# Hybrid decoder layer on one core: gating values computed token-major, and copies, residual additions, sums and a store placed elsewhere in the engines' programs

## The chip, the cores and the metric

The kernel runs on one core of a Trainium2 chip. The metric is the device time of one execution in microseconds (us). The engines are TensorE (PE, matrix products; PEld is its loading of stationary operands), VectorE (DVE), ScalarE (ACT), GpSimd (POOL) and SyncE (SP, which here only issues DMA transfers).

## The reference

A decoder layer over 512 tokens of width 2048, all in float32. What matters here:

```python
h = rmsnorm(x, norm_mix_g)
q, kv, nsa_g, u, v, merge_g = split(h @ w_in)          # v: 512 tokens x 1024
o_a = nsa_attention(...)                               # 16 heads
v = layernorm(gelu(v), ln_g, ln_b)                     # statistics over the 1024 values of a token
mixed = einsum('gts,bcsgd->bctgd', tril(ws), v)        # 8 groups of 128 values, chunks of 128 tokens
o_b = gelu(u) * (mixed + b)
x = x + (sigmoid(g0) * (o_a @ w_proj_a) + sigmoid(g1) * (o_b @ w_proj_b)) @ w_mix_out
x = x + cross_attention(rmsnorm(x), rmsnorm(mem))
gt, up = split(rmsnorm(x) @ w_ffn_in)                  # hidden width 5632
x = x + (silu(gt) * up) @ w_ffn_out
return rmsnorm(x, norm_final_g)
```

## The kernel before

**Precision.** Products are made in fp32r with both operands split into a high part and a low remainder: hi x hi, hi x lo and lo x hi are added in PSUM. ACT or DVE makes the high part (a copy to fp32r), DVE the remainder (a subtraction). A weight panel is 2048 x 128, loaded to `raw` in two slots and split by quarters (4 blocks of 128 rows) into `w_hi` and `w_lo`, which hold four quarters. PSUM has 8 banks of 128 x 512 float32.

**Order.** Each engine has its own program, written out by hand; semaphores tie them together, and a count says how far another engine must have come. An engine that waits holds everything behind it in its program. `Phase` keeps the counts: panels, quarters (`split_done` by DVE, `quarters_done` by PE) and groups (a group is one result in a bank, `banks_read` says that it was copied out). Most phases use banks 0 and 1 in turn.

**The stages that the change touches.**

- *merge, then sv.* While attention runs (banks 2 to 7), PE also makes 32 panels of merge gates in banks 0 and 1; ACT copies each to `gate_out`. Then phase `sv` computes v = h @ w_in[:, C_V:] in 8 panels of 128 features. The weights are stationary and the activations (`act_hi`, `act_lo`, 512 tokens) move, so a result has features on partitions and tokens along the row (`group`). ACT applies Gelu into `sv_t`. PE transposes it in four pieces, one panel later (`turn_v`, L1082), and ACT copies them to `v_rows` with tokens on partitions (`v_out`, L2073). After two panels PE also transposes the eight mixing matrices (`ws_rows`, L1093). DVE then takes the layer norm's statistics (`bn_stats`, L1513). In phase `su` PE computes u the same way, and one panel later mixes normalised v (`vn`, L1108), which ACT and POOL prepare.
- *f0, the plain part.* Three tile pairs (gate and up) of the first feed-forward product are made plainly. A loop over items, one for each quarter, runs in ACT and DVE: ACT `high` (L1880), DVE `low` (L1349), with other work between. `plain_up` (L2214) copies the up result, then waits for POOL's product `ff` (L2463) and issues its store (L2216).
- *Pairs.* The other 41 tile pairs use a seven-product scheme on 2 x 2 blocks (Strassen-Winograd): per pair 7 units of 24 products, whose weights are blocks or sums of blocks. `unit_high` and `unit_low` split a unit's weights two units ahead.
- *The output layer's runs.* The second feed-forward product uses the same scheme: 12 runs (`OUT_RUNS`) of 7 products. A run is cut into granules (`GRANULES`: run cb, product j, part q) of 12 matrix products of 128x512. The first two runs have 7 granules each, the others 14. `out_high` (ACT, L2264) and `out_low` (DVE, L1694) split the weights of a granule two granules ahead. `out_sum1` to `out_sum4` (L1702 to L1717) make the weight sums. A product j ends in a pair of banks. In the first two runs ACT copies some of them to `acc` (`keep`, L2268) and DVE adds others (`evacuate`, L1734); in later runs DVE adds all. PE starts a product only when its bank pair has been read. In runs 7 to 10 (`REST_AT`) PE also transposes a quarter of the residual into banks 6 and 7 (`turn_rest`, L1286), before products 2 and 4, and DVE adds it (`add_rest`, L1793); product 4 waits for the first addition, product 5 for the second.

Of the kernel before, what the change touches and what calls it, by code (L numbers as in the profile page):

```python
# [13 lines left out]
F32 = mybir.dt.float32  # L14
# [191 lines left out]
def build(nc, x, mem, norm_mix_g, w_in, cmp_pe_k, cmp_k_w1, cmp_k_b1, cmp_k_w2, cmp_pe_v, cmp_v_w1,  # L206
# [5 lines left out]
    with ExitStack() as ctx:  # L212
# [16 lines left out]
        w_lo = at("w_lo", [P, 4, 4, P], F32R, base + 24 * KIB)  # L229

# [40 lines left out]
        sv_t = at("sv_t", [P, 2, T], F32, C + 16 * KIB)  # L271
# [146 lines left out]
        v_turned = sem("v_turned")  # L418
        v_rows_done = sem("v_rows_done")
# [239 lines left out]
        def _(sp):  # L659
# [27 lines left out]
            columns(PH["sv"], w_in_v, C_V)  # L687
# [175 lines left out]
        def _(pe):  # L863
# [17 lines left out]
            def group(ph, i, u, hi, lo, n=T, m=P, extra=None, ready=None, low=None):  # L881
# [4 lines left out]
                wait(pe, banks_read, g - 1)  # L886
# [197 lines left out]
            def sgu_v(i):  # L1084
                for u in range(2):
                    group(ph, i, u, hi16, lo16)
                    if not (isinstance(i, int) and i == 0 and u == 0):
                        turn_v(i * 2 + u - 1, 1 - u)
            sgu_v(0)

            pe.wait_ge(ws_masked, 1)
            for g in range(SG):
                mm = pe.transpose(bank[4 + g // 4][:, (g % 4) * P:(g % 4 + 1) * P], ws_rows[:, g], ident[:])  # L1093
            mm.then_inc(ws_turned, 1)
            with pe.Fori(1, ph.n // 2) as i:
                sgu_v(i)
            turn_v(ph.n - 1, 1)


            ph = PH["su"]  # L1100
            pe.wait_ge(ws_ready, 2)
            def mix(n, u):
                pe.wait_ge(vn_done, n + 1)
                wait(pe, mix_copied, n - 1)
                if isinstance(n, int) and n < 2:
                    pe.wait_ge(v_rows_done, SG)
# [4 lines left out]
            def sgu_u(i):  # L1111
                for u in range(2):
                    group(ph, i, u, hi16, lo16)
# [204 lines left out]
        def _(dve):  # L1318
# [416 lines left out]
            for p in range(PAIRS):  # L1735
# [34 lines left out]
                if p + 1 < PAIRS:  # L1770
                    sum2(p + 1)
# [754 lines left out]
```

## Time and profile before

| | |
|---|---|
| median of 3 runs | 2844.76 us (2844.74 to 2845.18) |
| profiled execution | 2843.61 us, span 2841.8 us |
| mean granted TensorE clock | 0.997 of full speed |
| PE busy | 2773.9 us (98%) |
| DVE busy | 2032.8 us (72%) |
| ACT busy | 1048.9 us (37%) |
| POOL busy | 561.9 us (20%) |
| stage sv in the span | 822.4 to 914.5 us |
| stage f0 in the span | from about 1490 to 1558 us |
| output layer's runs in the span | 2385.0 to about 2827 us |

The span is the time from the first to the last instruction of the core. The profile takes one execution; its time is 1.15 us below the median. A matrix product's duration in the profile is longer than the distance to the next one, as they overlap: stages are measured from start to start.

### The profile page before, as it was taken

To read this page: it belongs to the slowest core of one execution; us is meant where nothing else is said; L and a number is where in the kernel's file an instruction comes from. 1 tells how busy PE (TensorE), PEld (TensorE's weight loads), DVE (VectorE), ACT (ScalarE), POOL (GpSimd) and SP (SyncE) were. 2 spreads that over 40 slices of the span, in tenths; PEclk is the share of its full clock that TensorE was granted. 3 is DMA by queue.
4 is the path that set the end of the run, shared out by engine and by line. 5 is a ranking of instruction groups with operands and counts; after the bars stand their busy time and mean duration, and the time that the engine had idled before them with its cause. 6 is when DMAs were issued, how large, how long until landed. Compare 5 with 4: busy or idle time off the path is not lost.

```text
span 2841.8 us, 42536 instructions
## 1 busy us (share of the span) xinstructions
PE 2773.9 (98%) x16343; PEld 2447.9 (86%) x16343; DVE 2032.8 (72%) x3061; ACT 1048.9 (37%) x1796; POOL 561.9 (20%) x471
## 2 busy tenths in 40 slices
PE   7999999999999999999989999999999999999997
PEld 6888778888888888888777999999999998888786
DVE  6544476776655555555677888898888887888887
ACT  6201254444421322211144444444444444443334
POOL 0200033343310555411000122122212221000000
PEclk9999999999999999999999999999999999999999
DMA  7632323323243445444244454655455547999972
GB/s 232 170 89 75 80 79 93 93 75 93 75 111 90 107 126 155 136 111 123 82 131 128 115 153 140 165 147 159 130 162 153 159 131 267 293 289 294 298 250 89
DMA packets 540964, 415.59 MB, mean 146 GB/s; under 512 B 12420, under 2 KB 488440, under 8 KB 534904
## 3 DMA queue, kind: packets, MB, share of 16 engines
q1 hardware_dynamic: 521968, 381.85, 45.5%
q0 software_dynamic: 5344, 10.49, 2.3%
q10 hardware_dynamic: 13480, 20.91, 2.2%
q8 instruction: 115, 1.88, 0.3%
q14 instruction: 57, 0.47, 0.0%
HBM read 354.22 MB, written 58.98 MB: 145 GB/s over the span
## 4 chain that ended last, share of the span: by engine, by line
PE 86%; DVE 5%; ACT 3%; issue 2%; POOL 2%; DMA 1%; ACTq 0%; DVEq 0%; POOLq 0%
PE banks L866 13%; PE banks L868 13%; PE banks L867 13%; PE banks L1252 10%; PE banks L1251 10%; PE banks L1250 10%; PE banks L1311 4%; PE banks L1312 4%; PE banks L1313 4%; PE banks L1029 1%; PE banks L1060 1%; PE banks L1045 1%; DMA rows_bc<-in_sgu_b_dram 1%; DVE w_lo L1330 1%; ACT wo_hi L2264 1%
## 5 line engine op out<-in xcount | busy, mean ns | idle before, releaser
L866 PE MATMUL banks<-act_hi,w_hi 128*128 128x512 f32 (+1 forms) x1360 | 540.2, 397 | 0.4 <-ACT gates L2007 0.4
L868 PE MATMUL banks<-act_hi,w_lo 128*128 128x512 f32 (+1 forms) x1360 | 531.3, 391 | 0.0
L867 PE MATMUL banks<-act_lo,w_hi 128*128 128x512 f32 (+1 forms) x1360 | 531.2, 391 | 0.0
L1328 DVE CAST w_hi<-raw 128x512 fp32r<-128x512 f32 x424 | 227.7, 537 | 368.1 <-PE banks L868 345.3
L1250 PE MATMUL banks<-t_hi,wf_hi 128*128 128x256 f32 x1312 | 371.3, 283 | 0.0
L1251 PE MATMUL banks<-t_lo,wf_hi 128*128 128x256 f32 x1312 | 371.3, 283 | 0.0
L1252 PE MATMUL banks<-t_hi,wf_lo 128*128 128x256 f32 x1312 | 371.3, 283 | 0.0
L1330 DVE TENSOR_TENSOR w_lo<-raw,w_hi 128x512 fp32r<-128x512 f32 x424 | 318.9, 752 | 14.5
L868 PEld LDWEIGHTS banks<-act_hi,w_lo 128*128 128x128 f32 (+1 forms) x1360 | 254.5, 187 | 56.6
L866 PEld LDWEIGHTS banks<-act_hi,w_hi 128*128 128x128 f32 (+1 forms) x1360 | 255.0, 187 | 45.5 <-ACT gates L2007 0.5
L867 PEld LDWEIGHTS banks<-act_lo,w_hi 128*128 128x128 f32 (+1 forms) x1360 | 255.2, 188 | 44.4
L1252 PE MATMUL banks<-tok_hi,wf_lo 128*128 128x256 f32 x984 | 278.5, 283 | 0.0
L1251 PE MATMUL banks<-tok_lo,wf_hi 128*128 128x256 f32 x984 | 278.5, 283 | 0.0
L1250 PE MATMUL banks<-tok_hi,wf_hi 128*128 128x256 f32 x984 | 278.5, 283 | 0.0
L1659 DVE TENSOR_TENSOR wf_lo<-raw_f,wf_hi 128x1024 fp32r<-128x1024 f32 x164 | 232.6, 1418 | 42.7 <-ACT wf_hi L2207 41.7
L1250 PEld LDWEIGHTS banks<-t_hi,wf_hi 128*128 128x128 f32 x1312 | 251.9, 192 | 0.0
L1251 PEld LDWEIGHTS banks<-t_lo,wf_hi 128*128 128x128 f32 x1312 | 251.9, 192 | 0.0
L1252 PEld LDWEIGHTS banks<-t_hi,wf_lo 128*128 128x128 f32 x1312 | 251.9, 192 | 0.0
L1311 PE MATMUL banks<-wo_hi,h_full 128*128 128x512 f32 x560 | 219.2, 391 | 5.0 <-DVE acc L1793 4.7
L1313 PE MATMUL banks<-wo_lo,h_full 128*128 128x512 f32 x560 | 218.0, 389 | 0.0
L1312 PE MATMUL banks<-wo_hi,h_full 128*128 128x512 f32 x560 | 217.9, 389 | 0.0
L2207 ACT ACTIVATE wf_hi<-raw_f 128x1024 fp32r<-128x1024 f32 x164 | 173.4, 1057 | 115.4 <-PE banks L1252 115.4
(314 smaller groups left out, 5424.3 us busy)
## 6 DMA issues: line engine op xcount, KB each, us to landing
raw_f<-in_w_ffn_in_dram SPq DMA_DIRECT2D x82, 1024.0 KB, 8.9
raw<-in_w_in_dram SPq DMA_DIRECT2D x68, 1024.0 KB, 5.6
h_full<-hidden_blocks SPq DMA_DIRECT2D x35, 1024.0 KB, 8.2
wo_raw<-in_w_ffn_out_dram SPq DMA_DIRECT2D x32, 1024.0 KB, 10.4
hidden_blocks<-tok_lo SPq DMA_DIRECT2D x44, 512.0 KB, 6.1
raw<-in_w_mix_out_dram SPq DMA_DIRECT2D x16, 1024.0 KB, 6.1
hidden_blocks<-h_hi SPq DMA_DIRECT2D x22, 384.0 KB, 2.5
hidden_blocks<-h_lo SPq DMA_DIRECT2D x22, 384.0 KB, 3.3
```

The source lines that it names most:

```text
L866: pe.matmul(dst, w_hi[:, q, j, 0:m], hi, start=first, stop=False)
L867: pe.matmul(dst, w_hi[:, q, j, 0:m], lo, start=False, stop=False)
L868: return pe.matmul(dst, w_lo[:, q, j, 0:m], hi, start=False, stop=last)
L1250: pe.matmul(dst, w_h[:, k], hi(k), start=start and k == 0, stop=False, skip_group_check=True)
L1251: pe.matmul(dst, w_h[:, k], lo(k), start=False, stop=False, skip_group_check=True)
L1252: mm = pe.matmul(dst, w_l[:, k], hi(k), start=False, stop=last, skip_group_check=True)
L1311: pe.matmul(dst, hi, wo_hi[g % 3][:, k], start=STARTS[j] and q == 0 and k == 0, stop=False, skip_group_check=True)
L1312: pe.matmul(dst, lo, wo_hi[g % 3][:, k], start=False, stop=False, skip_group_check=True)
L1313: mm = pe.matmul(dst, hi, wo_lo[g % 3][:, k], start=False, stop=last, skip_group_check=True)
L1328: dve.tensor_copy(w_hi[:, q, :, 0:width], src).then_inc(hi_done, 1)
L1330: dve.tensor_tensor(w_lo[:, q, :, 0:width], src, w_hi[:, q, :, 0:width].bitcast(F32), ALU.subtract).then_inc(split_done, 1)
L1659: dve.tensor_tensor(wf_lo[g % 3][:].rearrange("p k n -> p (k n)"), src, wf_hi[g % 3][:].rearrange("p k n -> p (k n)").bitcast(F32), ALU.su ...
```

## The change

- Phase `sv` computes v with activations stationary and weights moving. A load now brings 4 blocks of 128 rows by 512 features. Results have tokens on partitions: four banks (one for each 128 tokens) for features 0 to 511, four others for 512 to 1023. ACT applies Gelu from the banks straight into `v_rows`. The transposes, `sv_t` and the second copy are gone. PE first waits until all merge gates have been copied. DVE takes the statistics of the first half during `sv`.
- In the first two runs ACT copies banks (`keep`) before it makes the high part two granules ahead, not after; the one of the run's third granule is made ahead of the last Silu.
- In the four residual runs DVE does `add_rest` ahead of the granule's `out_low`.
- `out_sum1(0)` stands one subtraction and one addition earlier.
- The store of `ff` is issued two items later, the last one after two more splits in the first pair.

```diff
+        w_rows = [w[:].rearrange("p q j n -> p q (j n)") for w in (w_hi, w_lo)]
...
-            columns(PH["sv"], w_in_v, C_V)
+            ph = PH["sv"]
+            for n in range(ph.n):
+                i, u = ph.at(n)
+                b, k = divmod(n, 4)
+                sp.wait_ge(split_done, ph.quarter(i, u) - ph.nq)
+                sp.dma_start(raw[:, ph.slot(u)].rearrange("p (k a) n -> p k (a n)", a=4),
+                             w_in_v[:, 4 * k:4 * k + 4, C_V + b * T:C_V + (b + 1) * T]).then_inc(raw_landed[ph.slot(u)], 16)
...
-                wait(pe, banks_read, g - 1)
+                wait(pe, banks_read, g - 1 if free is None else free)
...
-            def turn_v(n, u):
-                pe.wait_ge(banks_read, ph.group0 + n + 1)
-                wait(pe, v_rows_done, n - 1)
-                for c in range(TC):
-                    mm = pe.transpose(bank[2 + u][:, c * P:(c + 1) * P], sv_t[:, u, c * P:(c + 1) * P], ident[:])
-                mm.then_inc(v_turned, 1)
...
+            def token_rows(n):
+                i, u = ph.at(n)
+                b, k0 = divmod(n, 4)
+                for q in range(4):
+                    k = 4 * k0 + q
+                    pe.wait_ge(split_done, ph.quarter(i, u) + q + 1)
+                    for c in range(TC):
+                        dst, rows = bank[4 * b + c][:], slice(c * P, (c + 1) * P)
+                        pe.matmul(dst, act_hi[:, k, rows], w_rows[0][:, q], start=k == 0, stop=False)
+                        pe.matmul(dst, act_lo[:, k, rows], w_rows[0][:, q], start=False, stop=False)
+                        mm = pe.matmul(dst, act_hi[:, k, rows], w_rows[1][:, q], start=False, stop=k == DK - 1)
+                    mm.then_inc(quarters_done, 1)
+            pe.wait_ge(banks_read, ph.group0)
+            pe.wait_ge(exp_done, ITEMS)
+            for n in range(ph.n):
+                if n == 2:
+                    pe.wait_ge(ws_masked, 1)
+                    for g in range(SG):
+                        mm = pe.transpose(bank[4 + g // 4][:, (g % 4) * P:(g % 4 + 1) * P], ws_rows[:, g], ident[:])
+                    mm.then_inc(ws_turned, 1)
+                if n == 4:
+                    pe.wait_ge(ws_ready, 2)
+                    pe.wait_ge(o_added, 2 * len(HALVES))
+                token_rows(n)
...
+            def row_stats(h):
+                dve.wait_ge(banks_read, PH["sv"].group0 + TC * (h + 1))
+                for c in range(TC):
+                    dve.bn_stats(bn[:, c, h], v_rows[:, c, h * 512:(h + 1) * 512]).then_inc(ln_stats, 1)
             for n in range(1, ph.n):
                 split(ph, *ph.at(n))
                 out_low(n - 1)
+                if n == 6:
+                    row_stats(0)
             ph = PH["su"]
             split(ph, 0, 0)
             out_low(SG - 1)
-
-            dve.wait_ge(v_rows_done, SG)
-            for c in range(TC):
-                for h in range(2):
-                    dve.bn_stats(bn[:, c, h], v_rows[:, c, h * 512:(h + 1) * 512]).then_inc(ln_stats, 1)
+            row_stats(1)
...
                 if p + 1 < PAIRS:
                     sum2(p + 1)
+                else:
+                    out_sum1(0)
                 ahead(5)
...
-                if p == PAIRS - 1:
-                    out_sum1(0)
...
+                if cb in REST_AT and j in (2, 4) and q == 1:
+                    add_rest(cb, j // 2 - 1)
                 if g + 2 < GRAN0[-1]:
                     out_low(g + 2)
...
-                if cb in REST_AT and j in (2, 4) and q == 1:
-                    add_rest(cb, j // 2 - 1)
...
+            def v_out(b):
+                act.wait_ge(quarters_done, ph.quarter0 + 16 * (b + 1))
+                for c in range(TC):
+                    act.activation(v_rows[:, c, b * T:(b + 1) * T], bank[4 * b + c][:], ACT.Gelu_apprx_tanh).then_inc(banks_read, 1)
...
+            def plain_store(i):
                 act.wait_ge(ff_done, i + 1)
                 act.dma_start(ff_dram[i * P:(i + 1) * P, :], ff[:]).then_inc(plain_kept, 16)
...
                 if q == 3 and n % 2 == 0:
                     plain_up(n // 2 - 1)
+                if q == 1 and n % 2 == 1 and n > 2:
+                    plain_store(n // 2 - 1)
...
                 ahead(1)
+                if p == 0:
+                    plain_store(PLAIN - 1)
...
+            out_high(UNITS + 2)
             act.wait_ge(joined, join_at(Z1, PAIRS - 1))
             act.activation(z[:], z[:], ACT.Silu).then_inc(z_silu, 1)
             LAST = len(OUT_RUNS) - 1
             for g, (cb, j, q) in enumerate(GRANULES, UNITS):
-                if g + 2 < GRAN0[-1]:
-                    out_high(g + 2)
                 if q == 0 and j > 0 and cb < 2 and j - 1 in BY_ACT:
                     keep(cb, j - 1)
                 if q == 0 and j == 0 and cb in (1, 2):
                     keep(cb - 1, 6)
+                if UNITS < g < GRAN0[-1] - 2:
+                    out_high(g + 2)
```

## Rows read from the trace of the kernel before

**Rows 1.** Page, busy us of an engine, share of the span, instructions.

```profile
PE 2773.9 (98%) x16343; PEld 2447.9 (86%) x16343; DVE 2032.8 (72%) x3061; ACT 1048.9 (37%) x1796; POOL 561.9 (20%) x471
```

**Rows 2.** Waits of PE, whole span: us in total, times, longest.

```profile
PE banks L1311 <- ACT acc L2268: 6.2, 3, 3.7
...
PE banks L1311 <- DVE acc L1793: 4.7, 4, 1.2
```

**Rows 3.** Waits of PE from 1470 to 1570 us.

```profile
PE banks L866 <- DVE w_lo L1349: 3.3, 2, 1.8
```

**Rows 4.** Timeline of PE in sv: start us, us, engine, line, operation [idle before].

```profile
850.08 0.39 PE L868 MATMUL banks<-act_hi,w_lo 128*128 128x512 f32 x1
...
856.20 0.39 PE L868 MATMUL banks<-act_hi,w_lo 128*128 128x512 f32 x1
...
856.78 0.48 PE L866 MATMUL banks<-act_hi,w_hi 128*128 128x512 f32 x1
...
913.24 0.60 PE L1082 MATMUL banks<-ident,sv_t 128*128 128x128 f32 x4
914.09 0.66 PE L1082 MATMUL banks<-ident,sv_t 128*128 128x128 f32 x4 [0.25 <-ACT sv_t L2079]
```

**Rows 5.** Timelines of ACT, POOL and PE ahead of sv and behind it.

```profile
822.62 0.60 ACT L2063 ACTIVATE gate_out<-banks 128x512 f32<-128x512 f32 x1 [3.04 <-PE banks L868]
...
928.09 1.29 POOL L2419 TENSOR_TENSOR vn<-vz,rows_bc 128x512 f32<-128x512 f32 x1
...
936.39 1.05 PE L1108 MATMUL banks<-ws_t,vn 128*128 128x128 f32 x8
```

**Rows 6.** Timelines of ACT, POOL, DVE and PE around the first store.

```profile
1519.38 0.58 ACT L2214 ACTIVATE up<-banks 128x512 f32<-128x512 f32 x1
...
1520.19 1.69 POOL L2463 TENSOR_TENSOR ff<-gated,up 128x512 f32<-128x512 f32 x1 [145.98 <-ACT up L2214]
...
1523.00 0.69 DVE L1349 TENSOR_TENSOR w_lo<-raw,w_hi 128x512 fp32r<-128x512 f32 x1 [2.27 <-ACT w_hi L1880]
...
1523.83 0.47 PE L866 MATMUL banks<-tok_hi,w_hi 128*128 128x512 f32 x1 [1.77 <-DVE w_lo L1349]
```

**Rows 7.** Timelines of PE, ACT, DVE and POOL in the first two runs.

```profile
2385.02 0.40 PE L1311 MATMUL banks<-wo_hi,tok_hi 128*128 128x512 f32 x1
...
2392.41 1.06 ACT L2264 ACTIVATE wo_hi<-wo_s 128x1024 fp32r<-128x1024 f32 x1 [2.62 <-DVE wo_s L1714]
2393.37 1.01 ACT L2268 ACTIVATE acc<-banks 128x1024 f32<-128x1024 f32 x1
...
2403.77 1.22 DVE L1734 TENSOR_TENSOR acc<-acc,banks 128x1024 f32<-128x1024 f32 x1 [0.34 <-PE banks L1313]
...
2416.59 0.69 PE L1311 MATMUL banks<-wo_hi,tok_lo 128*128 128x512 f32 x1 [1.99 <-ACT acc L2268]
...
2419.05 1.23 DVE L1694 TENSOR_TENSOR wo_lo<-wo_raw,wo_hi 128x1024 fp32r<-128x1024 f32 x1 [1.12 <-ACT wo_hi L2264]
...
2422.16 1.79 POOL L2474 TENSOR_TENSOR spare_lo<-h_rows 128x512 f32<-128x512 f32 x1
2422.37 2.68 DVE L1694 TENSOR_TENSOR wo_lo<-wo_raw,wo_hi 128x1024 fp32r<-128x1024 f32 x1 [2.09 <-ACT wo_hi L2264]
...
2423.74 0.39 PE L1311 MATMUL banks<-wo_hi,h_first 128*128 128x512 f32 x1
```

**Rows 8.** Window: length, busy of each engine (instructions), PEclk, DMA share, GB/s.

```profile
2418.00:2419.00 1.00, 1.00 (x4) 0.81 (x3) 0.00 (x0) 1.00 (x2) 0.00 (x0) 0.50 0.82 260
```

**Rows 9.** Timelines of DVE and PE in the first residual run.

```profile
2650.21 1.23 DVE L1694 TENSOR_TENSOR wo_lo<-wo_raw,wo_hi 128x1024 fp32r<-128x1024 f32 x1 [1.04 <-ACT wo_hi L2264]
2651.35 1.40 DVE L1793 SCALAR_TENSOR_TENSOR acc<-banks,ss,acc 128x512 f32<-128x512 f32 x2
2651.35 0.39 PE L1313 MATMUL banks<-wo_lo,h_full 128*128 128x512 f32 x1
...
2652.90 0.47 PE L1311 MATMUL banks<-wo_hi,h_full 128*128 128x512 f32 x1 [1.16 <-DVE acc L1793]
```

More of the change, by code:

```diff
@@ L270, in build @@
         v_rows = at("v_rows", [P, TC, 1024], F32, C)
-        sv_t = at("sv_t", [P, 2, T], F32, C + 16 * KIB)
         ut = at("ut", [P, 2, T], F32, C + 16 * KIB)
@@ L417, in build @@
         gate_stored = [sem("gate_stored0"), sem("gate_stored1")]
-        v_turned = sem("v_turned")
-        v_rows_done = sem("v_rows_done")
         ln_stats = sem("ln_stats")
@@ L879, in acts, with group @@
                 return act_hi[:, k], act_lo[:, k]
-            def group(ph, i, u, hi, lo, n=T, m=P, extra=None, ready=None, low=None):
+            def group(ph, i, u, hi, lo, n=T, m=P, extra=None, ready=None, low=None, free=None):
                 g = ph.group(i, u)
                 b = (ph.group0 + u) % 2
-                wait(pe, banks_read, g - 1)
+                wait(pe, banks_read, g - 1 if free is None else free)
                 if low is not None:
@@ L1077, in _ @@
             ph = PH["sv"]
-            def turn_v(n, u):
-                pe.wait_ge(banks_read, ph.group0 + n + 1)
-                wait(pe, v_rows_done, n - 1)
-                for c in range(TC):
-                    mm = pe.transpose(bank[2 + u][:, c * P:(c + 1) * P], sv_t[:, u, c * P:(c + 1) * P], ident[:])
-                mm.then_inc(v_turned, 1)
[L1084 to L1097, printed above, removed]
+            def token_rows(n):
[22 more added lines that the diff above has]
+                token_rows(n)
             ph = PH["su"]
-            pe.wait_ge(ws_ready, 2)
             def mix(n, u):
@@ L1105, in mix @@
                 if isinstance(n, int) and n < 2:
-                    pe.wait_ge(v_rows_done, SG)
+                    pe.wait_ge(banks_read, PH["sv"].groups_end())
                 for c in range(TC):
@@ L1112, in sgu_u @@
                 for u in range(2):
-                    group(ph, i, u, hi16, lo16)
+                    first = isinstance(i, int) and u == 0
+                    group(ph, i, u, hi16, lo16, free=PH["sv"].group0 + TC if first else None)
                     if not (isinstance(i, int) and i == 0 and u == 0):
@@ L2070, in _ @@
             ph = PH["sv"]
-            def v_out(n, u):
-                act.wait_ge(v_turned, n + 1)
-                act.activation(v_rows[:, :, ds(n * P, P)], bank[2 + u][:].rearrange("p (c f) -> p c f", c=TC), ACT.Copy).then_inc(v_rows_done, 1)
-            def sgu_v(i):
-                for u in range(2):
-                    n = i * 2 + u
-                    src = result(ph, i, u)
-                    wait(act, v_turned, n - 1)
-                    act.activation(sv_t[:, u], src[:], ACT.Gelu_apprx_tanh).then_inc(banks_read, 1)
-                    if not (isinstance(i, int) and n == 0):
-                        v_out(n - 1, 1 - u)
+            def v_out(b):
+                act.wait_ge(quarters_done, ph.quarter0 + 16 * (b + 1))
+                for c in range(TC):
+                    act.activation(v_rows[:, c, b * T:(b + 1) * T], bank[4 * b + c][:], ACT.Gelu_apprx_tanh).then_inc(banks_read, 1)
             for n in range(8):
                 act.activation(oa_hi[:, n], oa[:, n], ACT.Copy).then_inc(oa_hi_done, 1)
-            sgu_v(0)
             act.wait_ge(ws_turned, 1)
@@ L2087, in _ @@
                 act.activation(ws_t[:, 4 * h:4 * h + 4].rearrange("p g t -> p (g t)"), bank[4 + h][:], ACT.Copy).then_inc(ws_ready, 1)
-            with act.Fori(1, ph.n // 2) as i:
-                sgu_v(i)
-            v_out(ph.n - 1, 1)
+            v_out(0)
+            v_out(1)
             act.wait_ge(ln_stats, 3 * TC)
```

## The prediction

> **What bounds the kernel now.** I read the page first. TensorE (PE) is busy for 98% of the span [rows 1], so time can come only from fewer or shorter PE instructions and from PE's remaining idle gaps. Then I read the list of what PE waited for, whole and by stretch. Two waits belong to the output layer: PE on ACT's copies of banks (6.2 us in 3 waits, the longest 3.7) and PE on the residual addition at L1793 (4.7 us in 4 waits) [rows 2]. A third is the wait for split weights in the plain part of the first feed-forward product (3.3 us in 2 waits) [rows 3]. The list holds no wait of PE for a transfer in the output layer. Last I read timelines around each of those gaps and around the gating values (phase sv), and the granted clock in the output layer's first runs. Each edit of the change has its own place, so I price them one by one.
>
> **Gating values token-major.** Before, a panel is 48 products of 128x512 and then 4 transposes (L1082). The products start one per (856.20 - 850.08)/27 = 0.227 us [rows 4]. After, sv holds the same number: 8 panels x 4 quarters x 4 token chunks x 3 = 384, all 128x128 stationary by 512 moving. Only the roles are exchanged. I take the same 0.227 us for them, since weights and activations are tiles of one type and shape and both forms bring a weight load with each product. What goes is 8 x 4 transposes. From 856.20 to 856.78 a group of four adds 0.58 - 0.227 = 0.35 us, and the products just behind it start about 0.1 us late in sum (the first lasts 0.48 instead of 0.39), so 0.45 us a group and 3.6 us for eight. The last group also waits for the activation: 914.09 - 913.24 is 0.85 us, of which 0.35 are the transposes before it, so 0.5 us. Removed: 4.1 us.
>
> Added: sv now needs all four of banks 0 to 3 at once, so its first product waits for the last merge gate to be copied out of its bank. That copy runs from 822.62 to 823.21 [rows 5], whereas PE went straight on at 822.42. The wait is 0.9 us, with its late start behind it 1.0. Net: **3.1 us gained** (bounds 2.4 and 4.1).
>
> Hidden parts of this edit: ACT loses 8 copies of 0.6 us and has 8 Gelu evaluations in two bursts of four, each about 2.2 us. The first burst reads banks 0 to 3 while PE fills 4 to 7. The second is followed by four row statistics, not eight, so the normalisation ends earlier than before. It was not late before either: the first normalised group was finished at 929.38 and PE came to it at 936.39 [rows 5], so this gain is worth nothing. If that cover of 7 us were gone, PE would wait for the rest. SP's queue gets the same eight loads behind the same waits.
>
> **Store issued later.** ACT issues the store of the gated product right after the copy of `up` and waits there for POOL's multiply: the copy ends at 1519.96, POOL runs 1520.19 to 1521.88, and behind the waiting store stand ACT's next two splits. DVE's half of the split idles 2.27 us for them, until 1523.00, and PE idles 1.77 us until 1523.83 [rows 6]. With the store two items later, ACT splits at 1520.0, DVE at about 1520.8 (when its previous subtraction is done) and ends at 1521.4, and PE needs it at 1522.1. From there DVE runs about 2.25 us earlier against PE's 1.8, so no later item comes late; its narrowest margins grow from about 0 to 0.5 us. The same pattern at the second store costs 1.5 us. Sum 3.3 us [rows 3], and 0.5 us for slower restarts: **3.8 us gained** (bounds 2.3 and 3.8). The third store, moved past two splits, had no wait of PE behind it: 0. The buffer `ff` is next written at the following panel pair's multiply, a whole pair later.
>
> **First runs of the output layer.** ACT copies bank pairs out (`keep`, 1.01 us), and PE's next use of the pair waits for it. Before, the copy stands behind the split two granules ahead, and that split behind DVE's sums: granule 0 ended near 2387.9, yet ACT copied it at 2393.37, behind the split at 2392.41 [rows 7], and PE stood for 3.7 us. The other two waits of 0.5 and 2.0 us are the same. After the second long one the granted clock is 0.50 of 2.4 GHz, that is 1.2 GHz [rows 8], and the two granules from 2416.59 to 2423.74 take 7.15 us, where 24 products take 5.45: 1.7 us more.
>
> After the change I follow the three programs instruction by instruction from 2385.02, with 1.06 us for a high part in ACT, 1.01 for a copy, some 1.15 from one DVE instruction of 128x1024 to the next, and 2.73 us for a granule. The first sum starts about 2 us earlier, ahead of one subtraction and one short addition, so the second sum is done before granule 1 starts and granule 2's weights are ready at 2388.2. The copy of granule 0 runs at 2388.0 to 2389.0, as soon as the granule ends. PE then needs no stop up to granule 9. The bound is now DVE: granule 4 ends at 2385.02 + 5 x 2.73 + 0.2 = 2398.9, and DVE comes to the addition of its banks, which stood at 2403.77, at 2399.7: from the second sum at 2384.7 it has ten long instructions (11.5 us), two short ones (0.9 us) and 2.6 us of waits for ACT's high parts. From it to the end of the subtraction of 2419.05 the chain of sums, ACT's high parts and subtractions takes 16.5 us [rows 7], since ACT and DVE wait for each other there. That ends at 2416.3, and PE starts granule 11 then, after two short waits (0.4 and 0.7 us), instead of at 2423.74: 7.4 us.
>
> One thing speaks against the whole of it. DVE's subtraction at 2422.37 took 2.68 us beside POOL's sums, which began at 2422.16; the others of its form took 1.23 us [rows 7]. Before, PE was behind and did not notice. After, POOL's sums move to about 2417, again beside granule 12's subtraction, which would end near 2420.0 where PE wants it at 2419.05. I take 0.9 us for that. So **6.5 us gained** (bounds 4 and 8.7: without any wait granule 11 would start 30.0 us after 2385.02).
>
> By the Trainium skill's GPSIMD Engine Reference (section Specifications) GpSimd shares its SBUF interfaces with VectorE and contends with DVE instructions that have two SBUF inputs, as this subtraction has. By that rule the 0.9 us stays; by the plain duration of 1.23 us it would be 0 and the sum 0.9 us larger. The trace agrees with the rule at this one place.
>
> **Residual additions first.** In each of four runs the addition (1.40 us for two) stands behind a subtraction that waits for ACT until 2650.21; it runs from 2651.35, and PE's next product starts 1.55 us after its last instead of 0.227 [rows 9]. The transposes and the bank addition that it waits for lie a granule back, and DVE idles 1.04 us ahead of that subtraction, so first in its granule it runs 2649.1 to 2650.5, a microsecond before PE needs it at 2651.6. The subtraction then ends at 2651.7, for a granule due at 2654.3. The same swap two steps earlier delays a subtraction from 2638.6 to 2640.0, ending 2641.2 against a need at 2642.4. Gain 1.32 + 0.1 for the restart, four times: **5.6 us** (bounds 3 and 5.6).
>
> **Sum.** 3.1 + 3.8 + 6.5 + 5.6 = 19.0 us. The profiled execution took 2843.61 us around a span of 2841.8, so 2824.6 us by its own time. The median of the runs is 2844.76 us, so I predict 2825.8 us. About 0.2%, 5.7 us, is what a measurement of this kernel can tell from no change.
>
> **Rivals.**
> 1. Output start bound by something else. PE arrives about 5 us earlier at weights and hidden blocks loaded by SP, DMA engines are 82% busy in the row shown [rows 8], and DVE's chain may be slower than I traced. Then the 6.5 us shrink to 0 to 3: 2829 to 2832.5. For it: the DMA share. Against it: the list has no wait of PE on a transfer there, though it can't tell how much time was to spare. 14%.
> 2. A clock loss elsewhere. The new wait at the start of sv, or one of the old gaps that now falls at another moment, brings a stretch at 1.2 GHz of about 1.7 us, twice: 2829. It happened only after some gaps (the one of 3.7 us had none, that of 2.0 us had), so I can't place it. 7%.
> 3. The reordering doesn't do what it says: the copies and additions still end late because what they wait for (the granule's end, the transposes) is itself late, and sv's gain is eaten by its bank wait. Only a part of the store's 3.8 us is left: 2840 to 2845. Against it: the idle times before the instructions in rows 6, 7 and 9. 4%.
> 4. Slower: token-major products do not overlap their weight loads. Before, two of three consecutive products share w_hi as stationary; after, none do. Alone, a product lasts 0.39 us instead of its 0.227 pitch, and 384 x 0.164 = 63 us would be lost: 2889 us. It decides from a pitch of 0.227 + (15.9 + 5.7 + 3.1)/384 = 0.291 us. Against it: the first and second product of a triple, which share weights, start no closer together than the second and third. 2%.
>
> My forecast has 73%.
>
> **How the numbers follow.** Forecast's own range is 2823 to 2829: all upper bounds together (4.1 + 3.8 + 8.7 + 5.6 = 22.2) give 2822.6; the losses within it are 2 or 3 us at the output start. With rivals 1 and 2 the range is 2822.5 to 2832.5, which leaves rivals 3 and 4 and tails of the others outside. Faster by over 0.2%: 0.94. Within: 0.04. Slower: 0.02.
>
> **What would show it.** In sv: no L1082 and v_rows written from banks by Gelu eight times, a PE wait of about 0.9 us on the last gate copy, product pitch 0.227. In the plain part: the two waits on L1349 gone. At the output start: the waits of 3.7, 0.5 and 2.0 us replaced by at most 2 us on DVE's subtractions, and no stretch at 1.2 GHz. In the four residual runs: no wait on L1793. The prediction is wrong if sv is longer than 92 us, if a transfer appears among PE's waits, or if the DVE chain in the first two runs takes more than 16.5 us.

## The result and the profile after

Six runs of the changed kernel have a median of 2830.91 us (2829.69 to 2832.57), six of the kernel before 2845.11 us (2844.74 to 2847.77): ratio 0.995, 95% interval 0.994 to 0.996, 14.2 us less. The forecast was 19.0 us less, 2825.8 us. The measured time lies in the stated range (2822.5 to 2832.5), which the rivals widened, but above the 2823 to 2829 that I gave the forecast alone. The profiled execution after took 2829.69 us around a span of 2827.9, 13.9 us less span than before.

Where the 13.9 us are, in us, read from when PE starts the same product in both timelines. Nothing of the change lies ahead of sv, and there after is already 0.3 us early.

| product of PE | before | after | earlier by | gained in the stretch | forecast |
|---|---|---|---|---|---|
| last of the merge gates | 822.19 | 821.89 | 0.3 | | |
| first of su (behind sv) | 914.50 | 911.03 | 3.5 | 3.2 | 3.1 |
| start behind cross-attention's last wait | 1454.38 | 1451.47 | 2.9 | -0.6 | 0 |
| first block unit (behind the plain part) | 1558.47 | 1553.11 | 5.4 | 2.5 | 3.8 |
| granule 0 | 2385.02 | 2379.66 | 5.4 | 0 | 0 |
| granule 11 | 2423.74 | 2412.14 | 11.6 | 6.2 | 7.4 |
| granule 14 | 2431.91 | 2421.76 | 10.2 | -1.4 | -0.9 |
| behind the first residual transposes | 2634.25 | 2626.03 | 8.2 | -1.9 | 0 |
| last product | 2826.34 | 2812.49 | 13.9 | 5.6 | 5.6 |

The page's row of the engines, and PE's waits in the plain part and then in the first runs (us in total, times, longest), which answer to [rows 1 to 3]:

```profile
PE 2769.9 (98%) x16311; PEld 2444.3 (86%) x16311; DVE 2037.4 (72%) x3061; ACT 1044.8 (37%) x1788; POOL 561.8 (20%) x471
```

```profile
PE banks L870 <- DVE w_lo L1357: 0.8, 2, 0.5
```

```profile
PE banks L1319 <- DVE wo_lo L1704: 2.2, 3, 1.2
PE banks L1319 <- DVE acc L1744: 1.5, 2, 1.0
```

The three waits on ACT's bank copies and the four on residual additions [rows 2] are gone. In their place stand five on DVE, 3.7 us in all, and two, of 0.8 us in all, are left in the plain part.

**Gating values.** Timelines of PE and ACT after:

```profile
821.89 0.39 PE L872 MATMUL banks<-act_hi,w_lo 128*128 128x512 f32 x1
822.96 0.50 PE L1090 MATMUL banks<-w_hi,act_hi 128*128 128x512 f32 x1 [0.69 <-ACT gate_out L2073]
...
911.03 0.39 PE L870 MATMUL banks<-act_hi,w_hi 128*128 128x512 f32 x1
```

```profile
911.23 2.07 ACT L2084 ACTIVATE v_rows<-banks 128x512 f32<-128x512 f32 x4 [41.45 <-PE banks L1092]
```

The start is 1.07 us behind the product before it instead of 0.227: 0.84 us for the wait on the last gate copy, where the sum had 1.0. The 384 products then follow at 0.227 us, as in [rows 4]. ACT's last four Gelu evaluations end at 913.3 and PE waits for nothing behind them.

**The plain part.** Timelines of ACT, POOL, DVE and PE around the first store, answering to [rows 6]:

```profile
1516.52 0.58 ACT L2215 ACTIVATE up<-banks 128x512 f32<-128x512 f32 x1
1516.99 1.14 ACT L1890 ACTIVATE w_hi<-raw 128x512 fp32r<-128x512 f32 x2
```

```profile
1517.33 1.70 POOL L2470 TENSOR_TENSOR ff<-gated,up 128x512 f32<-128x512 f32 x1 [146.72 <-ACT up L2215]
```

```profile
1517.79 1.78 DVE L1357 TENSOR_TENSOR w_lo<-raw,w_hi 128x512 fp32r<-128x512 f32 x1
```

```profile
1519.72 0.47 PE L870 MATMUL banks<-tok_hi,w_hi 128*128 128x512 f32 x1 [0.53 <-DVE w_lo L1357]
```

The store no longer holds ACT's splits, and DVE's subtraction starts where the forecast put it (1520.8 less the 2.9 us by which PE is early here). But it takes 1.78 us; alone it takes 0.69 [rows 6]. It stands beside POOL's product, which ends at 1519.03; 1519.03 + 0.69 is 1519.72, and the subtraction ends at 1519.57. It looks as if POOL's product has taken the store's place as what makes PE wait, which an experiment below tests.

**The first runs.** DVE, POOL, ACT and PE after, answering to [rows 7]:

```profile
2391.07 2.33 DVE L1704 TENSOR_TENSOR wo_lo<-wo_first,wo_hi 128x1024 fp32r<-128x1024 f32 x1
...
2395.59 1.21 DVE L1744 TENSOR_TENSOR acc<-acc,banks 128x1024 f32<-128x1024 f32 x1
...
2410.86 1.23 DVE L1704 TENSOR_TENSOR wo_lo<-wo_raw,wo_hi 128x1024 fp32r<-128x1024 f32 x1 [1.13 <-ACT wo_hi L2268]
...
2414.99 2.66 DVE L1704 TENSOR_TENSOR wo_lo<-wo_raw,wo_hi 128x1024 fp32r<-128x1024 f32 x1
2417.57 1.21 DVE L1744 TENSOR_TENSOR acc<-acc,banks 128x1024 f32<-128x1024 f32 x1
```

```profile
2390.82 1.49 POOL L2495 TENSOR_TENSOR h_rows<-z,z_up 128x512 f32<-128x512 f32 x1 [19.77 <-DMA hidden_blocks<-h_lo]
2413.75 1.47 POOL L2477 DMA_DIRECT2D wo_s<-in_w_ffn_out_dram  x1 [21.43 <-DMA wo_s<-in_w_ffn_out_dram]
2414.76 1.80 POOL L2481 TENSOR_TENSOR spare_lo<-h_rows 128x512 f32<-128x512 f32 x1
2416.63 1.60 POOL L2483 TENSOR_TENSOR spare_lo<-h_rows,spare_lo 128x256 f32<-128x256 f32 x1
```

```profile
2426.20 2.01 ACT L2268 ACTIVATE wo_hi<-wo_s 128x1024 fp32r<-128x1024 f32 x2 [3.20 <-DMA wo_s<-in_w_ffn_out_dram]
```

```profile
2396.94 0.47 PE L1319 MATMUL banks<-wo_hi,h_first 128*128 128x512 f32 x1 [0.45 <-DVE acc L1744]
...
2418.92 0.47 PE L1319 MATMUL banks<-wo_hi,h_first 128*128 128x512 f32 x1 [1.01 <-DVE acc L1744]
...
2421.76 0.39 PE L1319 MATMUL banks<-wo_hi,h_full 128*128 128x512 f32 x1
...
2428.57 0.50 PE L1319 MATMUL banks<-wo_hi,h_full 128*128 128x512 f32 x1 [1.20 <-DVE wo_lo L1704]
```

Two subtractions beside POOL (2391.07 and 2414.99) take 1.1 and 1.4 us more than their 1.23; granules 6 and 13 wait for the additions behind them. The last wait (granule 16) looks like DVE's, but DVE waited for ACT and ACT until 2426.20 for a transfer: POOL's adding copy of the third run's summed weights, issued at 2413.75.

**Residual runs.** DVE after, answering to [rows 9]; the addition now comes first, and PE has no wait on it:

```profile
2640.79 1.41 DVE L1803 SCALAR_TENSOR_TENSOR acc<-banks,ss,acc 128x512 f32<-128x512 f32 x2
2642.11 1.22 DVE L1704 TENSOR_TENSOR wo_lo<-wo_raw,wo_hi 128x1024 fp32r<-128x1024 f32 x1
```

**Clock.** The stretch at 1.2 GHz of [rows 8] is gone: from 2380 to 2450 us the granted clock is 1.00 of 2.4 GHz. One is at another place, in cross-attention. Two of the products there stand 0.43 us apart, and the two windows of 10 us have granted clocks of 0.97 and 0.86:

```profile
1431.16 0.63 PE L871 MATMUL banks<-mo_lo,w_hi 128*128 128x512 f32 x1
1431.59 0.63 PE L872 MATMUL banks<-mo_hi,w_lo 128*128 128x512 f32 x1
```

```profile
1420.00:1430.00 10.00, 8.03 (x43) 6.37 (x42) 6.90 (x17) 1.62 (x5) 0.00 (x0) 0.97 0.00 0
1430.00:1440.00 10.00, 7.42 (x35) 5.44 (x34) 4.64 (x15) 2.18 (x7) 0.00 (x0) 0.86 0.37 107
```

### The profile page after: what moved, and what is told of

Same layout as the page of the kernel before. It is cut to its first block, busy times and chain, and to the rows that moved or that the text cites. A ratio compares the mean times of both kernels' runs of the same rounds, so it can differ in the third digit from the quotient of the medians.

```text
span 2827.9 us, 42359 instructions
## 1 busy us (share of the span) xinstructions
PE 2769.9 (98%) x16311; PEld 2444.3 (86%) x16311; DVE 2037.4 (72%) x3061; ACT 1044.8 (37%) x1788; POOL 561.8 (20%) x471
## 4 chain that ended last, share of the span: by engine, by line
PE 85%; DVE 6%; ACT 3%; DMA 2%; issue 2%; POOL 1%; ACTq 0%; DVEq 0%; POOLq 0%; SPq 0%
PE banks L870 12%; PE banks L872 12%; PE banks L871 12%; PE banks L1260 10%; PE banks L1259 10%; PE banks L1258 10%; PE banks L1319 4%; PE banks L1321 4%; PE banks L1320 4%; PE banks L1033 1%; PE banks L1090 1%; PE banks L1092 1%; PE banks L1091 1%; PE banks L1064 1%; PE banks L1049 1%
## 5 line engine op out<-in xcount | busy, mean ns | idle before, releaser
L870 PE MATMUL banks<-act_hi,w_hi 128*128 128x512 f32 (+1 forms) x1232 | 489.1, 397 | 0.4 <-ACT gates L2017 0.4
L871 PE MATMUL banks<-act_lo,w_hi 128*128 128x512 f32 (+1 forms) x1232 | 481.1, 390 | 0.0
L872 PE MATMUL banks<-act_hi,w_lo 128*128 128x512 f32 (+1 forms) x1232 | 480.9, 390 | 0.0
L872 PEld LDWEIGHTS banks<-act_hi,w_lo 128*128 128x128 f32 (+1 forms) x1232 | 230.2, 187 | 51.2
L870 PEld LDWEIGHTS banks<-act_hi,w_hi 128*128 128x128 f32 (+1 forms) x1232 | 230.6, 187 | 40.8 <-ACT gates L2017 0.5
L871 PEld LDWEIGHTS banks<-act_lo,w_hi 128*128 128x128 f32 (+1 forms) x1232 | 230.9, 187 | 39.6
```

Of the source, the lines that this page charges most:

```text
L870: pe.matmul(dst, w_hi[:, q, j, 0:m], hi, start=first, stop=False)
L871: pe.matmul(dst, w_hi[:, q, j, 0:m], lo, start=False, stop=False)
L872: return pe.matmul(dst, w_lo[:, q, j, 0:m], hi, start=False, stop=last)
```

## The experiments

**The four parts alone.** Each is the kernel before with one part of the change as its diff shows it: all of the token-major edit; the three `plain_store` hunks; `add_rest` ahead of `out_low`; the `keep` and `out_sum1(0)` hunks.

> The kernel before with only the token-major gating values. Theory (each edit acts in its own stage, and the total of 14.2 us is their sum): sv takes 88.9 us instead of 92.1, so 3.2 us faster, 2842 us, with one wait of about 0.7 us on the last gate copy. Rival (the changed moment of arrival brings a stretch at the lower granted clock in the cross-attention stage, as the kernel after shows at 1429 to 1432 us with 0.5 us lost): gain 2.6 us, with that stretch in this trace too. The prediction's rival of products that do not overlap their weight loads is excluded by the pitch of 0.227 us in the trace of after and should not show here either.

> The kernel before with only the later store. In the trace of after DVE's subtraction at 1517.79 took 1.78 us instead of 0.69, beside POOL's product of 1517.33, and PE still waited 0.5 and 0.2 us at the two places. Theory (DVE's two-input subtraction stands until POOL's product ends, then runs its own 0.69 us): 2.5 us faster, with the same two waits of 0.5 and 0.2 us and subtractions of about 1.8 us. Rival (what was left of the wait came from something that the other edits moved): the full 3.8 us and no wait of PE.

> The kernel before with only the residual additions ahead of the subtraction. Theory (independent): 5.6 us faster, 4 x 1.4, no wait of PE on the addition. Rival (in the kernel before these runs have other margins, and the displaced subtraction is late): less than 4 us, with waits of PE on DVE's subtraction in those runs.

> The kernel before with only the output layer's first runs changed (bank copies before splits, the first sum earlier). Theory (the same three limits as in the kernel after: POOL and DVE excluding each other twice, and the summed weights of the third run landing late): 2.9 us faster by the profile, with waits of PE of about 0.5, 0.6, 0.5, 1.0 and 1.2 us, the last on split weights whose transfer was issued by POOL. Rival (the interference comes from the shifts of the earlier stages): near the 6.5 us of the prediction. Rival 2 (nothing gained, all given back at the third run): under 1.5 us.

| part alone | median us | less than before (2845.03) | ratio, 95% interval |
|---|---|---|---|
| token-major | 2841.29 | 3.7 | 0.9987 (0.9978 to 0.9996) |
| later store | 2842.30 | 2.7 | 0.9992 (0.9983 to 1.0001) |
| residual additions | 2839.09 | 5.9 | 0.998 (0.9971 to 0.9989) |
| first runs | 2843.10 | 1.9 | 0.9995 (0.9986 to 1.0004) |

Medians of 11 runs each. They add up to 14.3 us, against 14.2 together, as parts that don't act on each other would. The times alone don't show it: each interval is 0.09% (2.6 us) to either side, and those of the store and of the first runs take in no change at all. The places of the products in the traces say it more finely. From cross-attention's last wait to the first block unit the store alone takes 101.6 us, as the kernel after does, against 104.1 before; from granule 0 to granule 11 the first runs alone take 32.46 us, against 32.48 after and 38.72 before. The token-major part alone reaches su at 911.29; its trace has the stretch at 1.2 GHz in cross-attention as well (granted clock 0.83 from 1430 to 1440 us). But so has the trace with the residual additions alone (0.83), where nothing differs ahead of that stage, and the one with the store alone has 0.89 from 1410 to 1420. The change isn't needed for that loss. The store alone leaves the same two waits, 0.8 us in all. The residual part brings the sum's 5.6 us in its trace: PE comes 0.7 us late to the first of the four runs, mostly from cross-attention, and the span is 5.0 us shorter. The first runs alone gained 1.9 us, less than the expected 2.9. Their waits from 2370 to 2440 us:

```profile
PE banks L1311 <- DVE wo_lo L1694: 3.5, 3, 2.5
PE banks L1311 <- DVE acc L1734: 1.8, 2, 1.3
```

The wait of granule 16 is 2.5 us here. The adding transfer, 9.1 us from issue to landing in the kernel before and 12.4 after, took 13.7 here.

**Product by DVE.** On the kernel after; the first hunk is in DVE's program, behind the item's split, the second in POOL's:

```diff
+                if item in (12, 20):
...
+                    dve.tensor_tensor(ff[:], gated[:], up[:], ALU.mult).then_inc(ff_done, 1)
...
-            for i in range(PLAIN):
+            for i in range(PLAIN - 1, PLAIN):
```

> The kernel after, with the gated product of the first two plain tiles computed by DVE, between two of its own instructions, instead of by POOL. Theory (POOL's product held DVE's subtraction for 1.1 us): the subtractions at about 1517.8 and 1540.2 us take 0.69 us, PE has no wait on them, and the time falls by 0.8 us of waits and 0.4 us of slower restarts, to about 2829.7 us, although DVE now does 0.6 us more. Rival (DVE was late anyway): the waits of 0.5 and 0.2 us stay or grow.

The median is 2829.05 us, 1.9 less than the kernel after. PE waits for nothing from 1500 to 1560 us, and from cross-attention's last wait to the first block unit it takes 100.5 us instead of 101.6. DVE's timeline:

```profile
1517.52 0.69 DVE L1357 TENSOR_TENSOR w_lo<-raw,w_hi 128x512 fp32r<-128x512 f32 x1
1518.12 0.68 DVE L1690 TENSOR_TENSOR ff<-gated,up 128x512 f32<-128x512 f32 x1
```

DVE does more and is earlier: without POOL's product the subtraction takes its 0.69 us and PE's two waits are gone. That the product was their cause is shown.

**Write only.** The kernel after with POOL's product left out, so its result is not the layer's; POOL writes a constant instead:

```diff
-                pool.tensor_tensor(ff[:], gated[:], up[:], ALU.mult).then_inc(ff_done, 1)
+                pool.memset(ff[:], 0.5).then_inc(ff_done, 1)
```

> The kernel after, with POOL's gated products of the plain tiles replaced by writing a constant to the same tile: the product is left out, POOL still writes but reads nothing. Theory (what excludes DVE is POOL reading SBUF while DVE reads two SBUF inputs, as the Trainium skill's page on SBUF, State Buffer, section on who interferes with whom, has it): DVE's subtractions beside it take 0.69 us. Rival (any POOL instruction holds DVE): they are prolonged by as long as the write lasts.

2830.1 us in one run. POOL's timeline at the first write:

```profile
1519.38 0.54 POOL L2470 MEMSET ff<- 128x512 f32 x1 [148.48 <-ACT up L2215]
```

DVE's there and in the first run of the output layer, then POOL's in that run:

```profile
1518.72 1.23 DVE L1646 TENSOR_TENSOR t_lo<-t_sum,t_hi 128x1024 fp32r<-128x1024 f32 x1 [0.53 <-ACT t_hi L2198]
...
2391.70 1.22 DVE L1704 TENSOR_TENSOR wo_lo<-wo_first,wo_hi 128x1024 fp32r<-128x1024 f32 x1
```

```profile
2391.84 2.25 POOL L2495 TENSOR_TENSOR h_rows<-z,z_up 128x512 f32<-128x512 f32 x1 [20.14 <-DMA hidden_blocks<-h_lo]
```

The write did not fall beside the subtraction that it was made for, which was over by then. It lay inside another one with two inputs in SBUF, and neither got longer; the second write (1540.54, 0.53 us) did so too. In both places DVE had come first, so a write that comes first isn't tested.

The other rows show what I had not foreseen: there DVE came 0.14 us ahead of POOL, and it is POOL's product that took 2.25 us, DVE's subtraction its plain 1.22. PE then had no wait up to granule 10, and granule 11 started 31.36 us behind granule 0 (2380.29 to 2411.65). In the kernel after POOL came 0.25 us ahead, and it was 32.48. The forecast had 31.3. All the other traces with this part of the change fall on one side or the other. DVE was ahead in two more, one of them by only 0.04 us (31.37 and 31.36 us to granule 11); POOL was in six more (32.46 to 32.48).

But the 1.1 us did not last. In the same trace granule 13 waited 2.1 us, and granule 14 came 42.0 us behind granule 0, against 42.1 in the kernel after. POOL's and DVE's rows there:

```profile
2414.32 1.47 POOL L2477 DMA_DIRECT2D wo_s<-in_w_ffn_out_dram  x1 [20.23 <-DMA wo_s<-in_w_ffn_out_dram]
2415.32 1.80 POOL L2481 TENSOR_TENSOR spare_lo<-h_rows 128x512 f32<-128x512 f32 x1
```

```profile
2414.50 3.71 DVE L1704 TENSOR_TENSOR wo_lo<-wo_raw,wo_hi 128x1024 fp32r<-128x1024 f32 x1
```

DVE's subtraction started 0.82 us ahead of POOL's first sum, but 0.18 us behind POOL's issue of the transfer, and yet stood until the sum was done. Coming earlier, DVE was only caught earlier.

**Sums in halves.** The transfers of the third run's summed weights, on SP's queue and on POOL's, in two halves; POOL's part is shown:

```diff
+                    if cb == 2:
+                        pool.wait_ge(s1_half, 16)
+                        pool.dma_start(w_sum(wo_s1, cb)[:, 0:2], fo_v[:, n:n + 3:2, f:f + OF], accum_op=ALU.add).then_inc(s1_half_added, 16)
+                        n, k0 = n + 4, 2
+                        pool.wait_ge(s1_copied, s1_at(cb))
```

> The kernel after, with the first two transfers of summed weights for the third run (copy by SP, adding copy by POOL) each issued as two halves with a semaphore of their own for the first half, which is all that granule 16 and the sum behind it need. Theory (granule 16 waits for this chain of transfers, landed at 2426.2 us): its wait of 1.2 us is gone and the time falls by about 1.4 us, 2829.5 us. Rival (the load of DMA engines as a whole is the limit, and the halves come no earlier): the wait stays near 1.2 us, no gain.

2827.40 us, ratio 0.9939 (0.9923 to 0.9956): 3.5 us less than the kernel after, 2.1 more than expected. Waits from 2370 to 2440 us:

```profile
PE banks L1324 <- DVE wo_lo L1709: 1.0, 2, 0.5
PE banks L1324 <- DVE acc L1749: 0.4, 1, 0.4
```

Both rows are of granules 6, 10 and 11. Granule 16 no longer waits, so the transfer was the cause, and the late starts up to 2450 us are gone as well. Granule 13's wait of 1.0 us went too, which I had not foreseen: POOL, released by the first half, began its sums at 2413.41 instead of 2414.76; the first of them fell for the most part beside DVE's addition of a bank (2413.61, its plain 1.21 us), and the subtraction behind it took 1.62 us instead of 2.66.

**POOL's sums held back.** POOL waits ahead of its block sums until DVE has made granule 15's subtraction; run on two chips, and once with only the second and third sum held back:

```diff
+                    if cb == 3:
+                        pool.wait_ge(f_lo, GRAN0[2] + 2)
```

> The kernel after, with POOL's block sums of 2414.76 us held back until DVE has made the subtraction for granule 15 (about 2422.4 us), where DVE idles 4.9 us. Theory (DVE's subtraction of 2414.99 us took 2.66 us because POOL's sum held it, and granule 13 waits for what follows): the subtraction takes 1.2 us, granule 13's wait of 1.0 us is gone, but granule 16's wait, which hangs on a transfer that this doesn't move, grows by as much, and the time stays within 0.3 us of the kernel after. Rival (the subtraction was slow for another reason, such as the traffic of that moment): 2.66 us again and the same wait at granule 13. Rival 2 (granule 16's wait is not fixed in time): 1.2 us faster.

> The kernel with only the sums held back, once more, on another chip. It was 2.8 us slower than the kernel after in the median, with the adding transfer started 4.8 us after its issue in the profile. Theory A (chance): this profile shows a start about 2 us after issue, and the time is within 0.7 us of 2830.9. Theory B (holding POOL's next instruction back makes the start late): 4 us or more again, and over 2832 us.

> The kernel after, with only the second and third of POOL's three block sums held back; the first, which reads SBUF for 1.8 us, follows the issue at once. Theory B (POOL's reading instruction right behind the issue is what lets the transfer be made ready): the transfer starts 2 us after issue, DVE's subtraction is held to about 2.7 us, granule 13 waits up to 1 us, and the time is that of the kernel after, 2831 us. Theory A (chance decides): no relation; a start of 2 us in the likeliest case, as in most of these transfers, and the same time, so that this run speaks for B only if the one before is slow.

2833.73 us (ratio 0.9957, 0.9941 to 0.9974) and 2833.95 us (0.996, 0.9946 to 0.9974) held back, 2830.56 us (0.9946, 0.9929 to 0.9962) with the first sum at once. The first two intervals overlap that of the kernel after, but eight of the nine runs are above 2832, and only one of the six after is. With all three held back granule 13's wait went as expected, and the subtraction took 1.22 us. (With the first sum at once the subtraction took 3.33 us and granule 13 waited 1.7, more than I expected. Here too DVE started between POOL's issue and its sum.) But granule 16 waited 8.7 us in the first profile and 4.1 in the second. The first profile is of an execution of 2838.31 us, 4.6 above its median, so its wait is not a typical one. Times of the adding transfer, from issue to landing: the kernel after, then the two with all sums held back, then the one with the first sum at once:

```profile
wo_s<-in_w_ffn_out_dram POOLq DMA_DIRECT2D x1, 1024.0 KB, 12.4
```

```profile
wo_s<-in_w_ffn_out_dram POOLq DMA_DIRECT2D x1, 1024.0 KB, 17.2
```

```profile
wo_s<-in_w_ffn_out_dram POOLq DMA_DIRECT2D x1, 1024.0 KB, 13.9
```

```profile
wo_s<-in_w_ffn_out_dram POOLq DMA_DIRECT2D x1, 1024.0 KB, 11.9
```

Holding back all three sums made the median 3 us longer, twice; why is not shown. The later landing can't be put down to it either: with the first runs alone, where nothing is held back, the transfer took 13.7 us. Its first packets came 4.8 us behind the issue in the first profile, but 2.0 in the second; with one sum at once they came 5.2 behind it, and it landed soonest of the three. In the kernel with the write only, where nothing is held back either, they came 4.8 us behind. So neither theory's sign, a late start, goes with the holding back or with the lateness. What remains open is whether POOL's reading, or the other transfers that an earlier granule 13 releases, decides. In both profiles PE's products behind the longer gap stand 0.43 us apart, the 1.2 GHz level. In the second granule 16 takes 4.4 us by it instead of 2.7.

**A better version.** The kernel after with the halves, the product on DVE, and the first products of sv in the order of the banks that come free:

```diff
+                    late = (ph.group0 - 1) % 2
-                    for c in range(TC):
+                    for c in (2, 3, 1 - late, late) if k == 0 and b == 0 else range(TC):
+                        if k == 0 and b == 0 and c == 1 - late:
+                            pe.wait_ge(banks_read, ph.group0 - 1)
+                        if k == 0 and b == 0 and c == late:
+                            pe.wait_ge(banks_read, ph.group0)
...
-            pe.wait_ge(banks_read, ph.group0)
```

> The kernel after with three mends: summed weights of the third run in halves, the gated product of the first two plain tiles on DVE, and the first token-major products in the order of banks 2, 3, then the one freed earlier, then the one that the last gate copy frees. Theory (each wait is local): no wait on the last gate copy (0.84 us with its late start), none on split weights in the plain part (1.3 us), none at granules 13 and 16 (2.6 us), so 4.7 us less than the span of 2827.9 us and, less the 0.4 us that a wait at granule 13 keeps, a time of about 2826.5 us. Rival (the earlier arrival meets late transfers again, as in the kernel with the sums held back): 2828 us or more, with a wait on split weights of over 1 us in the third run.

> The kernel with three mends, and POOL's block sums held back as well until DVE has made the subtraction for granule 15. Theory A (in the kernel with only the sums held back the adding transfer started 4.8 us after its issue by chance, as some of these transfers do in every kernel): the transfers here start about 2 us after issue and the time is that of the three mends within 0.5 us. Theory B (holding POOL's next instruction back delays the start of the transfer, because POOL's sum otherwise keeps DVE from holding the shared port while the transfer is made ready): the start is 4 us late or more again, and the time is 1 to 5 us above that of the three mends.

2825.38 us (ratio 0.9930, 0.9917 to 0.9944; 2826.5 expected) and, with the sums held back as well, 2825.51 us (0.9928, 0.9915 to 0.9942). The intervals touch that of the kernel after, but all ten runs (up to 2827.74) are below its lowest (2829.69). In the first, sv starts without a wait and the plain part has none; granule 13 waits 1.3 us again, since POOL's first sum, of 2411.26 (2.24 us), fell beside the subtraction of 2411.61, which took 2.99. In the second, granule 13 doesn't wait and granule 17, the first that needs the second half, waits 0.5 us; the queue's first packets come 2.0 us behind the first issue, as theory A has it, and the time is within its 0.5 us. With the halves, holding POOL back did no harm, and it brought nothing either.

## Why the prediction was right, and where it was not

The direction was right, and so was the mechanism of each of the four parts. The size was not: 14.2 us against 19.0. That the time lies in the stated range is owed to the room that rivals 1 and 2 had added to it, not to the sum. Of the signs that I had named, sv took 89.1 us (92 was the limit) and the DVE chain 16.5 us, as forecast (2395.59 to 2412.09); but the two waits of the plain part did not go, those on DVE in the first runs came to 3.7 us instead of at most 2, and a transfer did stand behind one of PE's waits, under DVE's name.

**Token-major.** Right in both terms: 3.2 us against 3.1, with 0.84 us for the bank wait against 1.0. The rival of products that don't overlap their loads is refuted by the pitch of 0.227 us from one product to the next.

**Store later.** The mechanism was right, the size not: 2.5 us against 3.8. The failing step is "DVE at about 1520.8", which "ends at 1521.4": it took the subtraction at its plain duration, 0.69 us, where 1.78 was measured. The store had kept DVE idle while POOL multiplied; with the store away the two meet. It cost DVE 1.1 us at each place, of which waits of 0.5 and 0.2 us, and slower restarts that I had counted as gained, came through to PE. With the product on DVE 1.1 of the missing 1.3 us came back.

**First runs.** The size was off: 2.9 us kept, against 6.5. Term by term: up to granule 11, 6.2 against 7.4. The chain of DVE was rightly followed (31.36 us where DVE came first, 31.3 forecast), and the 1.1 us missing there are POOL's product of 2390.82, which the sum had at nothing. From granule 11 to 14: 1.4 lost against 0.9, by the mechanism that I named, but one granule later: it prolonged the subtraction for granule 13, not 12, and PE waited for the addition of banks behind it. The two losses don't add up, though: in the write-only kernel, where POOL's product cost DVE nothing, the stretch from granule 11 to 14 took 1.0 us more, and granule 14 came 42.0 us behind granule 0 instead of 42.1. Only where the sums were held back as well did the 1.1 us stay (39.7 us where DVE came first, 40.8 where POOL did). From granule 14 on: 1.9 us lost where I had 0, of which 1.4 are granule 16's wait on the transfer, and the rest small late starts up to 2450 us, whose cause no run isolates. That PE "arrives about 5 us earlier at weights and hidden blocks" was in rival 1, at 14%; its mechanism did act, beside the forecast's, and its band (2829 to 2832.5) holds the measured time. The argument against it, that the list of before has no wait on a transfer, told nothing of the margin. It can be worked out: in the trace of before, issue 2421.15 and 9.1 us give 2430.3, and with 2.4 us from ACT's start to PE's (2426.20 to 2428.57 after) 2432.6; granule 16 started at 2437.3, so 4.7 us were to spare. PE came 10.2 us earlier, the transfer was issued only 7.4 earlier (2413.75 for 2421.15), and took 3.3 longer: 4.7 - 10.2 + 7.4 - 3.3 = -1.4, and granule 16 started 1.4 us late (2428.57, when 2427.2 was due).

**Residual additions.** 5.6 us, as forecast, four times 1.4.

**Clock.** The 1.7 us of the first runs came back as forecast. The 0.6 us lost in cross-attention is of the kind of rival 2, but such a loss appears in kernels without any edit ahead of it too.

The rule of the Trainium skill's page GPSIMD Engine Reference (section Specifications), which I had weighed at one subtraction for 0.9 us, was the right one; it held at four, two in the plain part and two in the first runs. The Trainium skill's page SBUF — State Buffer says more. By its section Who interferes with whom, a DVE instruction with two SBUF inputs contends with a GpSimd instruction that reads SBUF, not with one that only writes; by its section SBUF: two separate sides, the one that starts first has the shared interface for its whole instruction. The traces agree with the first, and with the second except behind an issue. DVE ended at 1519.57, 2393.40 and 2417.65, each 0.13 to 0.15 us short of POOL's end plus its own plain time, and POOL's 2.25 us is DVE's rest and its own 1.3. DVE's addition of a bank at 2417.57, with one input in PSUM, took its plain 1.21 us beside a sum of POOL. The two writes of a constant agree as well. Where DVE started between POOL's issue of a transfer and the sum behind it (0.18 us behind the issue in the write-only kernel, 0.56 with the first sum at once), it was held although it started ahead of the sum.

## What to carry to other kernels

When a wait goes, look at what the waiting engine will now run beside: an idle DVE hides a collision with POOL that the saved time then pays for. For each transfer that no one waits for, work out its margin (landing, and the work from there to the product) and compare it with how much earlier the product comes and how much earlier the transfer is issued; "no wait in the list" is not a margin. Splitting a transfer so that its first half releases the first user brought 3.5 us here; 1.0 of them came by the way, as POOL's sum moved off a subtraction. And follow a gain to the next meeting of the two engines: 1.1 us gained at granule 11 were gone at granule 14.

## What the runs showed of the hardware

- Where POOL's product met DVE's subtraction, the one that started first went first and the other waited for its end: with DVE ahead by 0.04 to 0.14 us POOL took 2.24 to 2.33 us and DVE 1.22, with POOL ahead by 0.13 us or more DVE took 2.3 us. Less than a quarter of a microsecond decided whether 1.1 us fell on the critical engine.
- A subtraction of DVE that started between POOL's issue of a transfer and POOL's sum behind it was held until the sum's end (3.71 and 3.33 us instead of 1.22); with the sums held back, one that started 1.2 us behind such an issue took its plain 1.22.
- An adding transfer of 1 MB issued by POOL took 9.1 to 17.2 us to land in the same place of nearly the same kernel, and the first packets of POOL's queue came 2.0 to 5.2 us behind the issue (by windows of 0.4 us). What it depends on stays open.
- Holding back POOL's arithmetic behind such an issue made the kernel 3 us slower, twice, though it removed the collision that it was meant to remove; with the transfer in halves it cost nothing.
